# Latent attention in a two-block model: score products split into rounded parts, and a diagonal of inverse sums in the turn of the exponentials

## The chip, the cores and the metric

One core of one Trainium2 chip runs the whole program, from the loads of the weights to the store of the result. The time is device microseconds (us) of one execution. TensorE (PE) multiplies, VectorE (DVE), ScalarE (ACT) and GpSimd (POOL) work elementwise, and SyncE (SP) issues the loads. The engines run side by side, each takes its own instructions in order, and they wait for each other by semaphores. PEld is TensorE's loading of the operand that stays in the array, which can overlap its products.

## The reference, cut to what matters

The model has a first block of two layers and a second, larger one. The change touches one part of each layer of the first block, the latent attention over 512 tokens with 8 heads, and nothing of the second block.

```
q = (rms_norm(c_q, q_norm_g) @ w_uq).reshape(B, S, MLA_HEADS, MLA_NOPE + MLA_ROPE)     # 64 + 32
q_nope, q_rope = q[..., :MLA_NOPE], apply_rope(q[..., MLA_NOPE:], cos, sin)
kv = (rms_norm(c_kv, kv_norm_g) @ w_ukv).reshape(B, S, MLA_HEADS, MLA_NOPE + MLA_V)
k_nope, v = kv[..., :MLA_NOPE], kv[..., MLA_NOPE:]
k_rope = apply_rope(k_r[:, :, None, :], cos, sin)[:, :, 0, :]
s = (einsum('bqhd,bkhd->bhqk', qn, k_nope) + einsum('bqhr,bkr->bhqk', qr, k_rope)) * scale
p = softmax(s, axis=-1)
o = einsum('bhqk,bkhd->bqhd', p, v)
```

All of it is in float32.

## The kernel before, in words

`first_block` runs each layer as stages with a barrier of all engines between them: `project_in`, `dilated_attention`, `mla_attention`, `project_out`. Whatever lengthens a stage's longest engine or chain lengthens the program.

`mla_attention` first makes q and k for all heads: products of halves (`low`, `uq`, `ukv`, in the type float32r, three products each for upper by upper, upper by lower and lower by upper part), a copy of q out of PSUM by ACT (L952), the turn by the rope tables on DVE (`turn`, L992), the inverse norms spread over a tile by a product with the identity (L899), and k times them on DVE (L1020). q and k (`qn`, `kn`, `qr`, `m.kr`) are then plain float32.

The rest of the stage is a loop over 16 units. A unit is a pair of heads (e = 0, 1) and a tile of 128 queries. Per unit:

- `score(u)`, PE: for each head one product over the 64 rows of the nope part (L830) and one over 32 rows of the rope part (L833), 512 keys wide. The two heads lie in different row groups of the array.
- DVE: the maximum (L1024) and the shift (L1025).
- ACT: the exponential with the row sum (L966), twice.
- DVE: the inverse of the sums (L1037) and the exponentials times it (L1039, "evened").
- `flip(u)`, PE: eight transposes of 128x128 (L852).
- ACT: copy of the transposed tiles out of PSUM (L974), twice.
- `mix(u)`, PE: sixteen short products with v (eight calls, L865).

PE's own order in the loop is written out by hand: `score(u + 1)`, `mix(u - 1)`, `flip(u)`. ACT's is the exponentials of u, then the copies of u - 1. DVE has, between the shift and the inverse of each unit, a quarter of a pair's `ada.fold` (class `Modulations`, L528 and L531): a vector times a weight matrix that a later stage needs. Its weights come in eight chunks of 1 MB per layer through a ring of four slots; SP issues the load of chunk n when the chunk that had the slot is folded (L509, L510). The unit with i == 1 also has one multiplication into `m.mix` (L1033), and after units 5, 9 and 13 PE sums the folded pair (`ada.sum`, L541).

Ahead of the loop PE runs score(0), value(0), value(1), score(1), value(2), value(3), where `value` makes v (L840) and ACT copies it out (L957).

Of the kernel before, what the change touches and what calls it, by code (L numbers as in the profile page):

```python
# [16 lines left out]
F32 = mybir.dt.float32  # L17
# [474 lines left out]
class Modulations:  # L492
# [6 lines left out]
    def __init__(self, nc, m, c, sem, layer, part, bank, held=2):  # L499
        self.nc, self.m, self.layer, self.part, self.bank, self.held = nc, m, layer, part, bank, held  # L500
        self.ring = c.enter_context(nc.sbuf_tensor(f"ada{part}_ring", [P, 4, KD, WC], F32))
        self.acc = c.enter_context(nc.sbuf_tensor(f"ada{part}_acc", [P, held, 2, WC], F32))
        self.loaded = [sem(f"ada_loaded{i}") for i in range(4)]
        self.own, self.folded, self.summed = sem("ada_own"), sem("ada_folded"), sem("ada_summed")

    def load(self, sp, chunks=range(ADA_CHUNKS)):
        for n in chunks:
            if n >= 4:
                sp.wait_ge(self.folded, n - 3)  # L509
            sp.dma_start(self.ring[:, n % 4], self.m.ada_w[bass.ds(self.layer, 1), self.part, n].rearrange(  # L510
                "l p k w -> p (l k) w")).then_inc(self.loaded[n % 4], 16)

    def fold(self, dve, pair, ks=range(KD)):
# [10 lines left out]
        for k in ks:  # L524
            for i in range(2):
                acc, w = self.acc[:, pair % self.held, i], self.ring[:, (2 * pair + i) % 4, k]
# [227 lines left out]
def mla_attention(nc, m, layer, gains):  # L754
# [6 lines left out]
    with stage(nc, "mla") as sem, ExitStack() as c:  # L761
# [5 lines left out]
        qn, qr = sb("qn", [P, PAIRS, T]), sb("qr", [P, 2, T])  # L767
# [3 lines left out]
        tmp, inv, spread = sb("tmp", [P, T]), sb("inv", [P, T]), sb("spread", [P, TT, P])  # L771
        rms, q_scale, q_minus = sb("rms", [P, 2, TT]), sb("q_scale", [P, TT]), sb("q_minus", [P, TT])
# [10 lines left out]
        ada = Modulations(nc, m, c, sem, layer, 1, m.ps[:, 7])  # L783
# [12 lines left out]
        with nc.Block(no_gpsimd_drain=True) as block:  # L796
# [14 lines left out]
            def _(pe):  # L811
                def score(u):
                    pair, i, s = u // TT, u % TT, 2 * (u % 2)
                    if u == 0:
                        pe.wait_ge(taken, 3)
                        pe.wait_ge(turned, 2)
                    elif i == 0:
                        pe.wait_ge(taken, 3 + pair)
                    if u == 2 * TT:
                        pe.wait_ge(turned, 3)  # L820
                    if i == 0:
                        pe.wait_ge(keyed, pair + 1)
# [5 lines left out]
                    for e in range(2):  # L828
                        h = halves(e)
                        nc.tensor.matmul(m.ps[:, s + e], qn[h, pair, at], kn[h, pair], start=True, stop=False)  # L830
                    for e in range(2):
                        r = slice(64 * e + 32 * (pair % 2), 64 * e + 32 * (pair % 2) + ROPE)
                        mm = nc.tensor.matmul(m.ps[:, s + e], qr[r, pair // 2, at], m.kr[r], start=False, stop=True)  # L833
# [2092 lines left out]
```

## Time and profile before

| | |
|---|---|
| median of 3 runs | 3000.61 us (2998.66 to 3001.7) |
| the profiled execution's own time | 2992.54 us |
| its span | 2990.7 us |
| share of the span: PE, PEld, DVE, ACT | 88%, 71%, 53%, 32% |
| mean granted TensorE clock | 0.917 of 2.4 GHz |
| latent attention, first work to last, first layer | 422.8 to 537.4 us |
| the same, second layer | about 1007 to 1127 us |

A share is an average over stages with different limits. The two stretches of latent attention together are some 235 us, 8% of the span. A float32 product stands in the trace as two records of PE, a float32r product and a transpose as one each.

### The profile page before, as it was taken

What the parts mean: (1) busy time and instruction counts of PE and PEld (TensorE: products, weight loads), DVE (VectorE), ACT (ScalarE), POOL (GpSimd) and SP (SyncE); (2) the same over time, 40 slices, a digit from 0 to 9 for tenths busy, and PEclk for the clock granted to TensorE, in tenths of its full rate; (3) what the DMA queues carried; (4) which work ended last, traced back from release to release, by engine and by line L of the source; (5) the groups of instructions that cost most, each with busy time, mean ns of one, the idle gap of its engine ahead of it and who ended that gap; (6) DMA issues with size and microseconds to landing.
All of it is one profiled execution on the core that took longest, in us unless ns stands there. A gap on an engine that the chain in (4) does not pass through costs nothing. (4 is left out here: it accounts for less than half of the span.)

```text
span 2990.7 us, 45168 instructions
## 1 busy us (share of the span) xinstructions
PE 2618.2 (88%) x19036; PEld 2109.0 (71%) x19036; DVE 1597.7 (53%) x2352; ACT 945.8 (32%) x1401; POOL 188.5 (6%) x163
## 2 busy tenths in 40 slices
PE   8999899889998998898663989589999892899998
PEld 7888675778886757687562878478878761688877
DVE  3473478835725687444556656644552348455532
ACT  4223135432231353423223333233332321433321
POOL 0000000200000002000001322010001000100001
PEclk9999999989999998899566999799999896899999
DMA  4332231423313214221001000222322120232231
GB/s 129 98 99 78 95 123 64 169 93 99 93 63 116 101 64 176 81 96 62 0 0 56 4 3 4 78 74 95 99 104 107 50 66 0 85 100 98 97 116 48
DMA packets 55958, 237.93 MB, mean 80 GB/s; under 512 B 6545, under 2 KB 7185, under 8 KB 47185
## 3 DMA queue, kind: packets, MB, share of 16 engines
q1 hardware_dynamic: 55760, 235.10, 23.3%
q8 instruction: 149, 2.44, 0.3%
q14 instruction: 49, 0.39, 0.0%
HBM read 230.88 MB, written 4.19 MB: 79 GB/s over the span
## 5 line engine op out<-in xcount | busy, mean ns | idle before, releaser
L341 PE MATMUL banks<-b_h,pin_pair 128*128 128x512 f32 x2304 | 528.3, 390 | 0.0
L341 PEld LDWEIGHTS banks<-b_h,pin_pair 128*128 128x128 f32 x2304 | 431.2, 188 | 88.9
L341 PE MATMUL banks<-ffh,ff_pair 128*128 128x512 f32 x2016 | 457.3, 389 | 0.0
L341 PEld LDWEIGHTS banks<-ffh,ff_pair 128*128 128x128 f32 x2016 | 378.4, 188 | 78.6
L341 PE MATMUL banks<-b_h,pab_pair 128*128 128x512 f32 x792 | 182.4, 393 | 8.0 <-DVE pab_pair L327 8.0
L341 PEld LDWEIGHTS banks<-b_h,pab_pair 128*128 128x128 f32 x792 | 149.9, 190 | 39.4 <-DVE pab_pair L327 8.2
L531 DVE SCALAR_TENSOR_TENSOR ada_acc<-ada_ring,sc,ada_acc 128x256 f32<-128x256 f32 x336 | 158.2, 538 | 0.0
L2558 DVE TENSOR_TENSOR ff<-ff_c,ff 128x512 fp32r<-128x512 f32 x44 | 30.5, 693 | 204.8 <-ACT ff L2546 203.4
L327 DVE TENSOR_TENSOR pin_pair<-pin_raw,pin_pair 128x1024 fp32r<-128x1024 f32 x50 | 61.3, 1226 | 141.4 <-ACT pin_pair L320 141.4
L1134 DVE SCALAR_TENSOR_TENSOR x<-banks,modf,x 128x512 f32<-128x512 f32 x32 | 24.0, 751 | 206.8 <-PE banks L359 206.8
L327 DVE TENSOR_TENSOR pin_pair<-first,pin_pair 128x1024 fp32r<-128x1024 f32 x50 | 61.3, 1226 | 125.2 <-ACT pin_pair L320 125.2
L320 ACT ACTIVATE ff_pair<-ff_raw 128x1024 fp32r<-128x1024 f32 x58 | 61.4, 1059 | 182.4 <-PE banks L341 182.4
L352 PE MATMUL banks<-ff,dn_pair 128*128 128x512 f32 x352 | 87.5, 406 | 13.9 <-ACT dn_pair L320 13.9
L352 PEld LDWEIGHTS banks<-ff,dn_pair 128*128 128x128 f32 x352 | 69.5, 198 | 29.6 <-ACT dn_pair L320 14.7
L320 ACT ACTIVATE dn_pair<-dn_raw 128x2816 fp32r<-128x2816 f32 x16 | 40.9, 2557 | 153.0 <-PE banks L359 142.1
L750 ACT ACTIVATE dil_pt<-banks 128x1024 f32<-128x1024 f32 x32 | 32.8, 1025 | 168.3 <-PE banks L676 168.3
L359 PE MATMUL banks<-ff,dn_pair 128*128 128x512 f32 x352 | 82.4, 389 | 0.0
L356 PE MATMUL banks<-ff,dn_pair 128*128 128x512 f32 x352 | 82.4, 389 | 0.0
L2256 DVE COPY_PREDICATED ru_inv<-rw_levels,banks 128x512 f32<-128x512 uint32 (+1 forms) x80 | 53.7, 676 | 53.2 <-PE banks L2085 52.7
L2686 DVE SCALAR_TENSOR_TENSOR fc_acc<-b_hb,params,fc_acc 128x512 f32<-128x512 f32 x116 | 76.9, 737 | 0.0
L356 PEld LDWEIGHTS banks<-ff,dn_pair 128*128 128x128 f32 x352 | 66.1, 188 | 13.7
L359 PEld LDWEIGHTS banks<-ff,dn_pair 128*128 128x128 f32 x352 | 66.1, 188 | 13.7
(496 smaller groups left out, 4604.2 us busy)
## 6 DMA issues: line engine op xcount, KB each, us to landing
ada_ring<-in_ada_w SPq DMA_DIRECT2D x48, 1024.0 KB, 7.8
ff_raw<-in_ffn_up SPq DMA_DIRECT2D x58, 512.0 KB, 3.7
pin_raw<-in_w_in SPq DMA_DIRECT2D x50, 512.0 KB, 3.6
first<-in_w_in SPq DMA_DIRECT2D x48, 512.0 KB, 3.6
dn_raw<-in_ffn_down SPq DMA_DIRECT2D x16, 1408.0 KB, 6.1
first<-in_ffn_up SPq DMA_DIRECT2D x30, 512.0 KB, 3.7
pab_raw<-in_ab_in SPq DMA_DIRECT2D x23, 512.0 KB, 3.5
out_raw<-in_w_out SPq DMA_DIRECT2D x12, 512.0 KB, 8.9
```

What stands on the lines that cost most here:

```text
L320: nc.scalar.activation(pair[:, t % slots, 0], ring.at(t), ACT.Copy).then_inc(rounded, 1)
L327: nc.vector.tensor_tensor(pair[:, t % slots, 1], ring.at(t), pair[:, t % slots, 0].bitcast(F32), ALU.subtract).then_inc(split, 1)
L341: mm = nc.tensor.matmul(bank, w(a, k), x(b, k), start=k == 0 and i == 0, stop=k == kt - 1 and i == 2)
L352: nc.tensor.matmul(bank, w(0, k), x(0, k), start=k == 0, stop=False)
L356: nc.tensor.matmul(bank, w(0, k), x(1, k), start=False, stop=False)
L359: mm = nc.tensor.matmul(bank, w(1, k), x(0, k), start=False, stop=k == kt - 1)
L531: ins = nc.vector.scalar_tensor_tensor(acc, w, self.m.sc[:, k:k + 1], acc, ALU.mult, ALU.add)
L750: nc.scalar.activation(pt[:, s:s + 2], m.ps[:, s:s + 2], ACT.Exp, scale=scale)\
L1134: ins = nc.vector.scalar_tensor_tensor(m.x[:, j], m.ps[:, j % 4], gate[:, j:j + 1], m.x[:, j], ALU.mult, ALU.add)
L2256: nc.vector.copy_predicated(inv[:, i % 2, f:2, e], over(m.levels[:, d, l, f:2]), m.ps[:, 4 + e, 2 * f * P:].rearrange("p (k t n) -> p k t ...
L2558: chain.step(nc.vector.tensor_tensor(ff[:, 1, j], cv[:, j % 2], ff[:, 0, j].bitcast(F32), ALU.subtract))
L2686: nc.vector.scalar_tensor_tensor(acc[:, k], hb[:, k, bass.ds(tap, T)], w[:, bass.ds(4 * tap + k, 1)], acc[:, k], ALU.mult, ALU.add).then_i ...
```

## The change

The scores: q and k are each split into an upper part (ACT copies the number into float32r, which rounds it) and a lower one (DVE subtracts the upper from the whole). Each float32 product becomes three float32r products, (upper, upper), (upper, lower), (lower, upper). The parts of k lie over `uq`, the parts of the rope pieces over `low`, both of which are no longer needed then.

The turn: DVE no longer multiplies the 128x512 exponentials by the inverse sums. It multiplies the 128x128 identity by them, and the eight transposes become eight float32 products of the exponentials with that diagonal.

The ring of the weight chunks in this stage has three slots in place of four.

```
-    def __init__(self, nc, m, c, sem, layer, part, bank, held=2):
+    def __init__(self, nc, m, c, sem, layer, part, bank, held=2, slots=4):
...
-            if n >= 4:
-                sp.wait_ge(self.folded, n - 3)
+            if n >= self.slots:
+                sp.wait_ge(self.folded, n - self.slots + 1)
...
-        qn, qr = sb("qn", [P, PAIRS, T]), sb("qr", [P, 2, T])
+        qn, qr = sb("qn", [P, 2, PAIRS, T], F32R), sb("qr", [P, 2, T])
+        kn_half = uq[:].rearrange("p a k n -> p (a k n)")[:, 0:2 * PAIRS * T].rearrange(
+            "p (a j n) -> p a j n", a=2, j=PAIRS)
+        kr_half, qr_half = low[:, :, 0], low[:, :, 1:3]
+        diag = spread[:].rearrange("p (u e) n -> p u e n", u=2)
-        ada = Modulations(nc, m, c, sem, layer, 1, m.ps[:, 7])
+        ada = Modulations(nc, m, c, sem, layer, 1, m.ps[:, 7], slots=3)
 # PE, score(u)
                     if u == 0:
-                        pe.wait_ge(taken, 3)
-                        pe.wait_ge(turned, 2)
+                        pe.wait_ge(rope_lower, 2)
+                    if u <= 1:
+                        pe.wait_ge(q_lower, PAIRS if u else 2)
                     if i == 0:
-                        pe.wait_ge(keyed, pair + 1)
+                        pe.wait_ge(k_lower, pair + 1)
-                    for e in range(2):
-                        h = halves(e)
-                        nc.tensor.matmul(m.ps[:, s + e], qn[h, pair, at], kn[h, pair], start=True, stop=False)
-                    for e in range(2):
-                        r = slice(64 * e + 32 * (pair % 2), 64 * e + 32 * (pair % 2) + ROPE)
-                        mm = nc.tensor.matmul(m.ps[:, s + e], qr[r, pair // 2, at], m.kr[r], start=False, stop=True)
+                    passes = ((0, 0), (0, 1), (1, 0))
+                    for a, b in passes:
+                        for e in range(2):
+                            h = halves(e)
+                            nc.tensor.matmul(m.ps[:, s + e], qn[h, a, pair, at], kn_half[h, b, pair],
+                                             start=(a, b) == passes[0], stop=False)
+                    for a, b in passes:
+                        for e in range(2):
+                            r = slice(64 * e + 32 * (pair % 2), 64 * e + 32 * (pair % 2) + ROPE)
+                            mm = nc.tensor.matmul(m.ps[:, s + e], qr_half[r, a, pair // 2, at], kr_half[r, b],
+                                                  start=False, stop=(a, b) == passes[2])
 # PE, flip(u)
-                            mm = nc.tensor.transpose(m.ps[:, 4 + e, j * P:j * P + P],
-                                                     ex[:, 2 * (u % 2) + e, j * P:j * P + P], m.ident[:])
+                            mm = nc.tensor.matmul(m.ps[:, 4 + e, j * P:j * P + P],
+                                                  ex[:, 2 * (u % 2) + e, j * P:j * P + P], diag[:, u % 2, e],
+                                                  start=j == 0, stop=j == TT - 1, skip_group_check=True)
 # PE, the products that make k
                     if j >= 2:
-                        pe.wait_ge(taken, j + 1)
+                        pe.wait_ge(q_lower, j - 1)
 # ACT, after the copy of the spread norms
+                act.wait_ge(turned, 1)
+                nc.scalar.activation(kr_half[:, 0], m.kr[:], ACT.Copy).then_inc(rope_upper, 1)
+                act.wait_ge(turned, 2)
+                nc.scalar.activation(qr_half[:, 0, 0], qr[:, 0], ACT.Copy).then_inc(rope_upper, 1)
+                for j in range(PAIRS):
+                    act.wait_ge(keyed, j + 1)
+                    nc.scalar.activation(kn_half[:, 0, j], kn[:, j], ACT.Copy).then_inc(k_upper, 1)
...
+                    if u == 2:
+                        act.wait_ge(turned, 3)
+                        nc.scalar.activation(qr_half[:, 0, 1], qr[:, 1], ACT.Copy).then_inc(rope_upper, 1)
 # DVE
+                def lower_rope(n, half, whole):
+                    dve.wait_ge(rope_upper, n + 1)
+                    nc.vector.tensor_tensor(half[:, 1], whole, half[:, 0].bitcast(F32), ALU.subtract)\
+                        .then_inc(rope_lower, 1)
...
                 turn(qr[:, 0])
+                lower_rope(0, kr_half, m.kr[:])
+                for t in range(PAIRS):
+                    dve.wait_ge(taken, 3 + t)
+                    nc.vector.tensor_tensor(qn[:, 1, t], m.ps[:, 2 + t], qn[:, 0, t].bitcast(F32), ALU.subtract)\
+                        .then_inc(q_lower, 1)
+                lower_rope(1, qr_half[:, :, 0], qr[:, 0])
...
                     nc.vector.tensor_tensor(kn[:, j], m.ps[:, k_bank(j)], inv[:], ALU.mult).then_inc(keyed, 1)
+                for j in range(PAIRS):
+                    dve.wait_ge(k_upper, j + 1)
+                    nc.vector.tensor_tensor(kn_half[:, 1, j], kn[:, j], kn_half[:, 0, j].bitcast(F32), ALU.subtract)\
+                        .then_inc(k_lower, 1)
...
+                    if u == 2:
+                        lower_rope(2, qr_half[:, :, 1], qr[:, 1])
...
                     for e in range(2):
-                        nc.vector.tensor_scalar(ex[:, s + e], ex[:, s + e], total[:, u % 2, e:e + 1], None, ALU.mult)\
-                            .then_inc(evened, 1)
+                        if u >= 2:
+                            dve.wait_ge(flipped, 2 * u + e - 3)
+                        nc.vector.tensor_scalar(diag[:, u % 2, e], m.ident[:], total[:, u % 2, e:e + 1], None,
+                                                ALU.mult).then_inc(evened, 1)
```

How the instructions stand, on the two engines that the loop waits for. First PE from score(1) into the loop, before: L830 and L833 are the scores, L840 makes v, L852 is the turn, L865 the products with v. The last number of a row is the count of calls.

```order
L830 MATMUL banks<-mla_raw,mla_qn 128x512 x2
L833 MATMUL banks<-b_kr,mla_qr 128x512 x2
L840 MATMUL banks<-mla_ukv,mla_low 128x512 x12
L852 MATMUL banks<-ident,mla_work 128x128 x8
L830 MATMUL banks<-mla_raw,mla_qn 128x512 x2
L833 MATMUL banks<-b_kr,mla_qr 128x512 x2
L865 MATMUL banks<-mla_work,mla_raw 64x128 x8
```

The same place after, where L839 and L844 are the scores (the upper and lower parts lie in `mla_uq` and `mla_low`), L852 makes v, L864 is the turn with the diagonal (in `mla_spread`) and L878 the products with v.

```order
L839 MATMUL banks<-mla_uq,mla_qn 128x512 x6
L844 MATMUL banks<-mla_low 128x512 x6
L852 MATMUL banks<-mla_ukv,mla_low 128x512 x12
L864 MATMUL banks<-mla_spread,mla_work 128x128 x8
L839 MATMUL banks<-mla_uq,mla_qn 128x512 x6
L844 MATMUL banks<-mla_low 128x512 x6
L878 MATMUL banks<-mla_work,mla_raw 64x128 x8
```

The order of the groups is the same; a score has twelve calls where it had four, and the turn keeps eight calls of another kind.

Now DVE from the end of the rope turn of the first q tile to the first maximum, before. L303 is the last step of a turn, L1020 is k times the norms, L1024 the maximum, L1025 the shift.

```order
L302 TENSOR_TENSOR mla_qr<-mla_qr,mla_cos 128x512
L303 TENSOR_TENSOR mla_qr<-mla_qr,mla_tmp 128x512
L1020 TENSOR_TENSOR mla_raw<-banks,mla_inv 128x512 x4
L1024 TENSOR_REDUCE mla_top<-banks 128x2
L1025 TENSOR_SCALAR mla_shift<-mla_top,mla_q_minus 128x2
```

And after: L1018 makes a lower rope part, L1049 the lower parts of q, L1055 is k times the norms, L1058 makes the lower parts of k, L1063 is the maximum.

```order
L303 TENSOR_TENSOR mla_qr<-mla_qr,mla_tmp 128x512
L1018 TENSOR_TENSOR mla_low<-b_kr,mla_low 128x512
L1049 TENSOR_TENSOR mla_qn<-banks,mla_qn 128x512 x4
L1018 TENSOR_TENSOR mla_low<-mla_qr,mla_low 128x512
L1055 TENSOR_TENSOR mla_raw<-banks,mla_inv 128x512 x4
L1058 TENSOR_TENSOR mla_uq<-mla_raw,mla_uq 128x512 x4
L1063 TENSOR_REDUCE mla_top<-banks 128x2
```

Ten subtractions have come in ahead of the first maximum; score(0) on PE waits for the first seven of them and for all four multiplications of k.

## Rows read from the trace of the kernel before

**Rows 1.** The page: busy time, share and instructions of each engine.
```profile
PE 2618.2 (88%) x19036; PEld 2109.0 (71%) x19036; DVE 1597.7 (53%) x2352; ACT 945.8 (32%) x1401; POOL 188.5 (6%) x163
```
**Rows 2.** The windows view, loops of both layers; PEclk is the granted clock.
```profile
core 0: us, PE busy (x) PEld busy (x) DVE busy (x) ACT busy (x) POOL busy (x), PEclk, DMA share, GB/s
469.10:530.00 60.90, 59.99 (x468) 34.69 (x467) 56.26 (x127) 35.45 (x83) 0.00 (x0) 1.00 0.21 79
1059.60:1120.00 60.40, 57.85 (x451) 33.51 (x451) 54.50 (x124) 35.25 (x82) 0.00 (x0) 1.00 0.21 79
```
**Rows 3.** The timeline, PE, one unit: start, duration, engine, line, xrecords.
```profile
476.35 1.13 PE L830 MATMUL banks<-mla_raw,mla_qn 64*128 64x512 f32 x4
477.41 1.13 PE L833 MATMUL banks<-b_kr,mla_qr 32*128 32x512 f32 x4
478.48 1.09 PE L865 MATMUL banks<-mla_work,mla_raw 128*64 128x128 f32 x16
479.51 1.09 PE L852 MATMUL banks<-ident,mla_work 128*128 128x128 f32 x8
480.53 1.13 PE L830 MATMUL banks<-mla_raw,mla_qn 64*128 64x512 f32 x4
```
**Rows 4.** The timeline, DVE and ACT, the same unit; idle time in brackets.
```profile
478.59 1.23 DVE L1024 TENSOR_REDUCE mla_top<-banks 128x2 f32<-128x1024 f32 x1
479.98 0.61 DVE L528 TENSOR_SCALAR ada_acc<-ada_ring,sc 128x256 f32<-128x256 f32 x2
480.11 0.78 ACT L966 ACTIVATE mla_work<-banks,mla_shift,mla_q_scale 128x512 f32<-128x512 f32 x1 [1.68 <-DVE mla_shift L1025]
481.64 1.08 ACT L974 ACTIVATE mla_work<-banks 128x512 f32<-128x512 f32 x2
481.77 0.17 DVE L1037 RECIPROCAL mla_total<-mla_total 128x2 f32<-128x2 f32 x1 [0.39 <-ACT mla_work L966]
481.97 0.88 DVE L1039 TENSOR_SCALAR mla_work<-mla_work,mla_total 128x512 f32<-128x512 f32 x2
```
**Rows 5.** The timeline, PE weight loads: score(3) and the last score, first layer.
```profile
472.05 0.30 PEld L830 LDWEIGHTS banks<-mla_raw,mla_qn 64*128 64x128 f32 x4 [0.17 <-issue]
525.21 0.30 PEld L830 LDWEIGHTS banks<-mla_raw,mla_qn 64*128 64x128 f32 x4
```
**Rows 6.** The timeline ahead of the loop: float32r and float32 products, a small scaling.
```profile
436.92 0.86 DVE L1007 TENSOR_SCALAR mla_spread<-ones,mla_rms 128x128 f32<-128x128 f32 x4
435.90 8.47 PE L892 MATMUL banks<-mla_low,mla_uq 128*128 128x512 f32 x36
443.99 1.08 PEld L899 LDWEIGHTS banks<-ident,mla_spread 128*128 128x128 f32 x8
444.99 5.30 PEld L911 LDWEIGHTS banks<-mla_low,mla_ukv 128*128 128x128 f32 x24
```
**Rows 7.** The timeline, the start of the first layer's loop.
```profile
446.80 0.68 DVE L1020 TENSOR_TENSOR mla_raw<-banks,mla_inv 128x512 f32<-128x512 f32 x1
450.64 0.30 PEld L830 LDWEIGHTS banks<-mla_raw,mla_qn 64*128 64x128 f32 x4 [0.35 <-issue]
460.87 0.69 ACT L957 ACTIVATE mla_raw<-banks,mla_rms 128x512 f32<-128x512 f32 x1 [0.67 <-PE banks L840]
462.88 0.78 ACT L966 ACTIVATE mla_work<-banks,mla_shift,mla_q_scale 128x512 f32<-128x512 f32 x1
465.28 1.61 PE L852 MATMUL banks<-ident,mla_work 128*128 128x128 f32 x8 [4.44 <-DVE mla_work L1039]
```
**Rows 8.** The timeline, the last turn of the first layer.
```profile
532.65 1.09 PE L852 MATMUL banks<-ident,mla_work 128*128 128x128 f32 x8
```
**Rows 9.** The tile view of the ring, 476.9 to 477.4 us: one load.
```profile
L510 SPq DMA_DIRECT2D ada_ring<-in_ada_w x1: 333/333/333, 477.1 to 477.1; - x1
DMA to landing us min/median/max: 4.8/4.8/4.8
```
**Rows 10.** The windows view, stretches at the lower clock in and behind both loops.
```profile
465.70:469.10 3.40, 3.40 (x13) 1.57 (x12) 3.21 (x8) 2.05 (x6) 0.00 (x0) 0.50 0.02 5
1049.40:1059.60 10.20, 8.78 (x37) 5.11 (x38) 7.75 (x18) 4.48 (x11) 0.00 (x0) 0.50 0.01 2
537.40:544.20 6.80, 4.70 (x10) 2.88 (x11) 5.42 (x8) 6.17 (x10) 0.00 (x0) 0.50 0.77 277
1121.10:1134.70 13.60, 9.98 (x41) 7.36 (x40) 6.51 (x11) 7.36 (x12) 0.00 (x0) 0.50 0.40 149
```

More of the change, by code:

```diff
@@ L497 @@
     PAIRS = ADA_CHUNKS // 2
-    def __init__(self, nc, m, c, sem, layer, part, bank, held=2):
+    def __init__(self, nc, m, c, sem, layer, part, bank, held=2, slots=4):
         self.nc, self.m, self.layer, self.part, self.bank, self.held = nc, m, layer, part, bank, held
-        self.ring = c.enter_context(nc.sbuf_tensor(f"ada{part}_ring", [P, 4, KD, WC], F32))
+        self.slots = slots
+        self.ring = c.enter_context(nc.sbuf_tensor(f"ada{part}_ring", [P, slots, KD, WC], F32))
         self.acc = c.enter_context(nc.sbuf_tensor(f"ada{part}_acc", [P, held, 2, WC], F32))
-        self.loaded = [sem(f"ada_loaded{i}") for i in range(4)]
+        self.loaded = [sem(f"ada_loaded{i}") for i in range(slots)]
         self.own, self.folded, self.summed = sem("ada_own"), sem("ada_folded"), sem("ada_summed")
@@ L507, in load @@
         for n in chunks:
-            if n >= 4:
-                sp.wait_ge(self.folded, n - 3)
-            sp.dma_start(self.ring[:, n % 4], self.m.ada_w[bass.ds(self.layer, 1), self.part, n].rearrange(
-                "l p k w -> p (l k) w")).then_inc(self.loaded[n % 4], 16)
+            if n >= self.slots:
+                sp.wait_ge(self.folded, n - self.slots + 1)
+            sp.dma_start(self.ring[:, n % self.slots], self.m.ada_w[bass.ds(self.layer, 1), self.part, n].rearrange(
+                "l p k w -> p (l k) w")).then_inc(self.loaded[n % self.slots], 16)
     def fold(self, dve, pair, ks=range(KD)):
@@ L525, in fold @@
             for i in range(2):
-                acc, w = self.acc[:, pair % self.held, i], self.ring[:, (2 * pair + i) % 4, k]
+                acc, w = self.acc[:, pair % self.held, i], self.ring[:, (2 * pair + i) % self.slots, k]
                 if k == 0:
@@ L766, in mla_attention @@
         low = sb("low", [P, 2, nq + nkv, T], F32R)
-        qn, qr = sb("qn", [P, PAIRS, T]), sb("qr", [P, 2, T])
+        qn, qr = sb("qn", [P, 2, PAIRS, T], F32R), sb("qr", [P, 2, T])
+        kn_half = uq[:].rearrange("p a k n -> p (a k n)")[:, 0:2 * PAIRS * T].rearrange(
+            "p (a j n) -> p a j n", a=2, j=PAIRS)
+        kr_half, qr_half = low[:, :, 0], low[:, :, 1:3]
+        q_lower, rope_upper, rope_lower, k_upper = (
+            sem(x) for x in ("q_lower", "rope_upper", "rope_lower", "k_upper"))
+        k_lower = sem("k_lower")
         v, kn = (raw[:, n * TT * T:(n + 1) * TT * T].rearrange("p (j n) -> p j n", j=TT) for n in range(2))
@@ L814, in score @@
                     if u == 0:
-                        pe.wait_ge(taken, 3)
-                        pe.wait_ge(turned, 2)
-                    elif i == 0:
-                        pe.wait_ge(taken, 3 + pair)
+                        pe.wait_ge(rope_lower, 2)
+                    if u <= 1:
+                        pe.wait_ge(q_lower, PAIRS if u else 2)
                     if u == 2 * TT:
-                        pe.wait_ge(turned, 3)
+                        pe.wait_ge(rope_lower, 3)
                     if i == 0:
-                        pe.wait_ge(keyed, pair + 1)
+                        pe.wait_ge(k_lower, pair + 1)
                     if u == 1:
@@ L951, in _ @@
                     act.wait_ge(made, t + 1)
-                    nc.scalar.activation(qr[:, t] if t < 2 else qn[:, t - 2], m.ps[:, t], ACT.Copy).then_inc(taken, 1)
+                    nc.scalar.activation(qr[:, t] if t < 2 else qn[:, 0, t - 2], m.ps[:, t], ACT.Copy)\
+                        .then_inc(taken, 1)
                 act.wait_ge(stretched, 1)
                 nc.scalar.activation(inv[:], m.ps[:, 7], ACT.Copy).then_inc(spread_in, 1)
+                act.wait_ge(turned, 1)
[5 more added lines that the diff above has]
+                    nc.scalar.activation(kn_half[:, 0, j], kn[:, j], ACT.Copy).then_inc(k_upper, 1)
                 for i in range(TT):
```

## The prediction

> **What bounds the kernel now.** I read the page's busy shares first, then the windows of the two loops, then the timeline of one unit engine by engine, and last the starts and ends of the stage. TensorE is busy 88% of the span [rows 1], which says little of this stage; the windows do: in both loops of the latent attention PE is busy 96 to 98% at the full clock, DVE over 90%, ACT under 60% [rows 2]. The timeline of a unit shows PE without a hole: the nope scores start at 476.35, the rope scores 1.06 us later, the products with v 1.07 after that, the turn 1.03 later, the next score 1.02 later; 4.18 us in all [rows 3]. The reader is to see the second thing, too: DVE and ACT run almost as long a cycle. Counted from the end of the score (478.48), the maximum starts at +0.11, the fold at +1.50, the exponentials at +1.63, the copies run from +3.16 to +4.24, the inverse stands at +3.29, and the two multiplications of the exponentials end at +4.37 [rows 4]. So the loop has two nearly equal bounds, and the change lengthens one and shortens the other. From score(3) to the last score there are twelve intervals in 53.16 us [rows 5], 4.43 each, since three of them hold an `ada.sum` of PE's. The rest of the program isn't touched.
>
> **The scores.** A float32 product is two records, and the two heads' products lie in different row groups: four records of 512 columns take 1.06 us [rows 3]. Two heads side by side would need 2 x 2 x 512 columns at 2.4 GHz, 0.85 us, so 0.21 us are left for the first weight load and the change of tile shape. The float32r products of the q projection take one record each, and 36 of them go from 435.90 to 443.99, 0.225 us each [rows 6]. They use all 128 rows; no row shows float32r products of 64 or 32 rows. I take the value by which they pair up as the float32 ones do, since the calls alternate e = 0 and e = 1 and lie in different banks: three rounds of 0.225 plus 0.21 make 0.885 us in place of 1.06. Both kinds of score together: 1.77 in place of 2.13, a saving of 0.36 us. The lower bound is rounds of 0.213, a saving of 0.43; the upper is that the heads go one after the other, twelve times 0.225 plus 0.42, 3.12 us, 0.99 us more than before.
>
> A rule speaks against my value. The hidden loads show in the rows: 36 full-height products with 36 loads pass at 0.225 us each, with one load of 128 columns behind every one of them [rows 6]. The Trainium skill, page "TensorE: Matmul & The Clock Gate", Part 3, says that a weight load overlaps a running product only when its row group differs. By that rule the second and third round of each score show their loads and the saving is gone; by the row it stands. The trace contradicts the rule for full height, and shows nothing for half height in float32r. I keep it as rival A.
>
> **The turn.** Eight transposes, one record each, take 1.02 us [rows 3]. The product that spreads the norms has the form of the new turn (float32, 128x128 against a 128x128 moving tile): eight records for four products, 1.00 us from its first load to the next product's [rows 6], of which about 0.11 is the change, so 0.111 a record. Eight products are sixteen records, eight more than now: +0.89, with the slightly longer records of this form +0.91 us. The unit on PE becomes 4.18 - 0.36 + 0.91 = 4.73 us.
>
> **DVE and ACT in the loop.** Scaling four 128x128 tiles took 0.86 us [rows 6], so a diagonal costs 0.22 and the two 0.43 in place of 0.88. They end at +3.92 in place of +4.37, and the next score ends at +4.73: DVE gets 0.8 us of slack. The copies end at +4.24 and the products with v may start at +4.73: 0.49 us of slack. The saving on DVE is therefore worth nothing; its cover is PE's longer unit. The new wait of DVE on `flipped` is for the turn two units back, long done. The single subtraction and copy of the third rope piece at u = 2 (0.69 and 0.6 us) fit into the slack but for 0.1 or 0.2 us.
>
> **The ring of three.** Chunk 3 can be asked for only when chunk 0 is folded, near the end of unit 3, where it was there from the start; the same for chunks 5 and 7 at units 7 and 11. The next fold waits for it, and behind that wait on DVE stand the inverse, the diagonal and the next maximum. A load issued in this place landed 4.8 us later [rows 9]. The chunk is free about 1.3 us into the fold, so it is there 1.3 + 0.2 + 4.8 = 6.3 us after that fold began, and the next fold comes 4.73 after it: DVE stands for 1.6 us. The fold then ends at 1.50 + 1.6 + 1.5 = +4.6, the diagonals at +5.25. The turn wants them at 4.73 + 1.03 = +5.76: in time. The next maximum is 0.4 us late, the copies have 0.49: also in time. Price 0, with nothing left; each us by which a chunk comes later costs a us at six places.
>
> **The start of the loop.** Score(0) waits for seven new subtractions and four multiplications on DVE. From 446.80, eleven operations of 0.68 plus 0.03 between them [rows 7] end at 454.8 by steps of 0.72; before, score(0) started at 450.64 [rows 7], since the multiplications were waiting for PE anyway. That is +4.2. PE gets back 2 x 0.36 on scores 0 and 1: the last v copy (460.87) and the first exponential (462.88) [rows 7] come 3.5 later. The first turn (465.28) waits for half a multiplication before and a diagonal now, 0.26 less: +3.2. The other three subtractions of k and ACT's six copies lie beside score(0) and the products for v.
>
> **The sum, per layer.** Start +3.2. First turn +1.2 (0.91, but part of it at the lower clock, which began at 465.70 and 1049.40 [rows 10]). Interval from score(2) to score(3), at the lower clock in part, +0.7. Twelve intervals of +0.55, less some 0.3 us that PE waits now: +6.3. End: last score -0.36, last turn (532.65 [rows 8]) +0.91, both on the path: +0.5. Together 11.9, and 23.8 for two layers. Against the profiled execution: 2992.5 + 23.8 = 3016.3. The median of the runs shown lies 8.1 above that execution, and I forecast medians: 3000.6 + 23.8 = 3024.
>
> **The rivals.**
> A, the loads show. Four rounds a unit pay half of the 0.21, about 0.11, and are 0.213 long otherwise: +0.36 a unit, sixteen units, two layers, +11.5: 3036. For it: nothing in float32r at half height is in the trace. Against: the full-height row.
> B, the heads go one after the other in float32r: 1.35 a unit more than forecast, +43: 3067. Against: the float32 products of the same shape do pair up.
> C, the chunks come later than 4.8 us after the issue: 2 us more at six places, +12: 3036. The slack is used up by my own sum, which speaks for it; that two loads issued 0.5 us apart share the same engines is in the 4.8 already.
> D, the clock gives it back, which would end without a loss. The place is the start and end of both loops: 3.4, 10.2, 6.8 and 13.6 us stand at half clock [rows 10], 34 us, of which all with PE work would be worth half, 17 us: 3007; with rounds of 0.213 in all units 2.3 less, 3005, within the measurement. It decides from about 18 us given back. For it: the turns become true products, and the first half-clock stretch begins in a turn. Against: both loops ran at the full clock for 60 us with transposes in them [rows 2], and the idle time ahead of the first turn stays. The Trainium skill, same page, Part 4, says that transposes don't count as work for the clock as products do. By that rule the new turns would help to hold the clock; the trace shows no lower clock in a running loop that they could lift.
> E, the clock takes more. PE has nothing to do between the end of k's products, about 451.1, and 454.8. The idle 4.4 us ahead of the first turn [rows 7] was followed by a lower clock [rows 10]; if this new hole is too, 3.4 us at half clock cost 1.7 a layer and 10.2 cost 5: 3028 to 3034.
>
> **How the numbers follow.** Forecast 0.57 (its own range 3016 to 3033), E 0.15, A 0.09, B 0.08, C 0.05, D 0.06. The range of 3012 to 3042 takes in the forecast, E, A and C, alone and A with E; B and D stay out. What a measurement of this kernel can tell from no change is about 0.2%, 6 us. Half of D and a little luck in the forecast's low end make 0.04 for the same, 0.03 for faster; all else is slower, 0.93.
>
> **What would show it.** In the profile after: the nope and rope scores start 0.88 us apart, not 1.06 (A), not 1.5 (B). The turns show sixteen records and 1.93 us. Starts of scores in the loop are 4.73 us apart, PE over 97% busy there. The first turn comes 3.2 us later in its stage. DVE stands 1.6 us ahead of the fold at units 4, 8 and 12 and PE doesn't. Granted clock in both loops 1.00. The forecast is wrong if the time is under 3012, if PE waits in the loop, or if the scores are longer than 1.77 us.

## The result, and the profile after

The changed kernel takes 3023.91 us (median of 4, 3020.27 to 3026.57), the kernel before on the same chip 2999.64 (median of 4, 2997.69 to 3001.7). The ratio is 1.008, with an interval of 1.0063 to 1.0097: slower by 24.3 us, where 24 was forecast. The profiled execution has a span of 3024.8 us.

The page, busy time by engine, answers to [rows 1]: PE has 22 us more, DVE 1 and ACT 8.

```profile
PE 2640.0 (87%) x19382; PEld 2160.4 (71%) x19420; DVE 1598.8 (53%) x2374; ACT 954.3 (32%) x1415; POOL 188.3 (6%) x163
```

The windows of both loops answer to [rows 2], with the same columns: PE 97% busy, DVE down from 92% to 71% in the first layer, the granted clock 1.00 in both. The 3% are two waits behind the last score (540.45); up to there PE doesn't stand.

```profile
477.50:551.00 73.50, 71.59 (x674) 56.68 (x674) 52.45 (x130) 37.67 (x86) 0.00 (x0) 1.00 0.21 80
1078.30:1151.80 73.50, 71.59 (x674) 56.66 (x674) 52.46 (x130) 37.67 (x86) 0.00 (x0) 1.00 0.22 80
```

The timeline of PE, one unit, answers to [rows 3]. L839 and L844 are the nope and rope scores, L878 the products with v, L864 the turn.

```profile
485.32 0.97 PE L839 MATMUL banks<-mla_uq,mla_qn 64*128 64x512 f32 x6
486.22 0.96 PE L844 MATMUL banks<-mla_low 32*128 32x512 f32 x6
487.11 1.09 PE L878 MATMUL banks<-mla_work,mla_raw 128*64 128x128 f32 x16
488.13 2.05 PE L864 MATMUL banks<-mla_spread,mla_work 128*128 128x128 f32 x16
490.12 0.96 PE L839 MATMUL banks<-mla_uq,mla_qn 64*128 64x512 f32 x6
```

From start to start that is 0.90, 0.89, 1.02 and 1.99 us, a unit of 4.80 where it was 4.18. There is no idle time in brackets: PE has no hole. The six records of a score stand for three rounds of two heads, the sixteen of the turn for eight float32 products.

DVE and ACT around the same unit, at the fold whose chunk comes late (they answer to [rows 4]):

```profile
490.31 0.62 DVE L529 TENSOR_SCALAR ada_acc<-ada_ring,sc 128x256 f32<-128x256 f32 x2 [1.60 <-DMA ada_ring<-in_ada_w]
490.27 1.08 ACT L998 ACTIVATE mla_work<-banks 128x512 f32<-128x512 f32 x2
491.83 0.48 DVE L1082 TENSOR_SCALAR mla_spread<-ident,mla_total 128x128 f32<-128x128 f32 x2
491.90 1.09 PE L878 MATMUL banks<-mla_work,mla_raw 128*64 128x128 f32 x16
492.92 2.05 PE L864 MATMUL banks<-mla_spread,mla_work 128*128 128x128 f32 x16
```

DVE stood for 1.60 us, yet the diagonals (491.83, 0.48 long) are done 0.6 us before the turn starts. The first layer's waits of DVE on the ring, from the view of waits (us in total, times, longest):

```profile
DVE ada_acc L529 <- DMA ada_ring<-in_ada_w: 4.7, 3, 1.6
```

The timeline of the start of the loop answers to [rows 7]:

```profile
448.49 0.68 DVE L1018 TENSOR_TENSOR mla_low<-b_kr,mla_low 128x512 fp32r<-128x512 f32 x1
449.09 2.48 DVE L1049 TENSOR_TENSOR mla_qn<-banks,mla_qn 128x512 fp32r<-128x512 f32 x4
451.48 0.68 DVE L1018 TENSOR_TENSOR mla_low<-mla_qr,mla_low 128x512 fp32r<-128x512 f32 x1
452.08 2.48 DVE L1055 TENSOR_TENSOR mla_raw<-banks,mla_inv 128x512 f32<-128x512 f32 x4
454.48 2.49 DVE L1058 TENSOR_TENSOR mla_uq<-mla_raw,mla_uq 128x512 fp32r<-128x512 f32 x4
455.27 0.90 PEld L839 LDWEIGHTS banks<-mla_uq,mla_qn 64*128 64x128 f32 x6 [2.86 <-issue]
```

The first lower part of k (454.48) is the last of the eleven DVE operations, counted from 448.49, that score(0) needs; score(0) starts 0.79 us behind its start. The eleven step by 0.60 us. The windows of the two stretches at the lower clock in this layer, same columns as above (they answer to [rows 10]):

```profile
455.40:462.20 6.80, 6.80 (x21) 4.60 (x22) 5.14 (x10) 0.69 (x1) 0.00 (x0) 0.50 0.00 0
472.50:475.90 3.40, 3.40 (x18) 3.17 (x18) 3.21 (x9) 2.17 (x6) 0.00 (x0) 0.50 0.02 5
```

The first begins with score(0), behind a hole on PE: for 2.86 us it loaded no weights, for 2.46 it ran no product. Before, there was no such stretch at this place. The second begins in the first turn, as before.

From the barrier ahead of the latent attention to the one behind it, the two layers took 114.9 and 121.0 us before, and 130.6 and 130.5 after: +15.6 and +9.5, 25.1 together. By the prediction's terms, in us:

| term | forecast, a layer | layer 1 | layer 2 |
|---|---|---|---|
| up to the first copy of q (unchanged code) | 0 | +1.5 | 0.0 |
| from there to score(0) | +4.2 | +3.0 | +3.0 |
| score(0) to the first turn | -1.0 | +2.2 | +2.2 |
| first turn to score(2) | +1.2 | +1.9 | +1.7 |
| score(2) to score(3) | +0.7 | -0.4 | -2.6 |
| twelve intervals | +6.3 | +6.8 | +6.8 |
| last score to the end | +0.5 | +0.6 | -1.6 |
| sum | 11.9 | 15.6 | 9.5 |

The +1.5 is not the change's. In the 26 layers of all the profiles of this document, the way from the start of the stage to the first copy of q takes 18.2 to 18.3 us where the clock is at half for 10.2 us around the stage's start, and 19.5 to 19.7 where it is so for 13.7. The kernel before had 10.2 in its first layer and 13.7 in its second, the changed kernel 13.7 in both.

The profiled spans differ by 34.1 us, the medians by 24.3. Of the 34.1, 9.0 lie outside the two stages, in code that is the same; single executions scatter by that much (the kernel before alone ran in 2976.8 to 2998.3 us on one chip). So below, stages and units are read from profiles, and medians only beside the runs of the kernel before on the same chip.

### The profile page after: what moved, and what is told of

The parts are those of the page before. It is cut to its first block and busy times, and to the rows that moved or that the text cites. A ratio compares the mean times of both kernels' runs of the same rounds, so it can differ in the third digit from the quotient of the medians.

```text
span 3024.8 us, 45962 instructions
## 1 busy us (share of the span) xinstructions
PE 2640.0 (87%) x19382; PEld 2160.4 (71%) x19420; DVE 1598.8 (53%) x2374; ACT 954.3 (32%) x1415; POOL 188.3 (6%) x163
## 3 DMA queue, kind: packets, MB, share of 16 engines
HBM read 230.88 MB, written 4.19 MB: 78 GB/s over the span
## 5 line engine op out<-in xcount | busy, mean ns | idle before, releaser
L352 PEld LDWEIGHTS banks<-ff,dn_pair 128*128 128x128 f32 x352 | 69.5, 198 | 29.7 <-ACT dn_pair L320 14.7
L864 PE MATMUL banks<-mla_spread,mla_work 128*128 128x128 f32 x512 | 68.7, 290 | 8.5 <-DVE mla_spread L1082 8.5
L359 PEld LDWEIGHTS banks<-ff,dn_pair 128*128 128x128 f32 x352 | 66.1, 188 | 13.7
```

Of the source, the lines that this page charges most:

```text
L352: nc.tensor.matmul(bank, w(0, k), x(0, k), start=k == 0, stop=False)
L359: mm = nc.tensor.matmul(bank, w(1, k), x(0, k), start=False, stop=k == kt - 1)
L864: mm = nc.tensor.matmul(m.ps[:, 4 + e, j * P:j * P + P], ex[:, 2 * (u % 2) + e, j * P:j * P + P], diag[:, u % 2, e], start=j == 0, stop=j ...
```

## The experiments

Two edits come back below: the old turn (the exponentials scaled by DVE, then transposed) and a ring of four.

**The scores alone.** The changed kernel with the old turn, the ring still three chunks long.

```diff
-                            mm = nc.tensor.matmul(m.ps[:, 4 + e, j * P:j * P + P],
-                                                  ex[:, 2 * (u % 2) + e, j * P:j * P + P], diag[:, u % 2, e],
-                                                  start=j == 0, stop=j == TT - 1, skip_group_check=True)
+                            mm = nc.tensor.transpose(m.ps[:, 4 + e, j * P:j * P + P],
+                                                     ex[:, 2 * (u % 2) + e, j * P:j * P + P], m.ident[:])
...
-                        nc.vector.tensor_scalar(diag[:, u % 2, e], m.ident[:], total[:, u % 2, e:e + 1], None,
-                                                ALU.mult).then_inc(evened, 1)
+                        nc.vector.tensor_scalar(ex[:, s + e], ex[:, s + e], total[:, u % 2, e:e + 1], None, ALU.mult)\
+                            .then_inc(evened, 1)
```

> The changed kernel with the old turn: DVE multiplies the exponentials, PE transposes; scores in three rounds and ring of three stay. Theory (the new turn is PE's cost, the split scores save a third of a us a unit there): PE's share of a unit falls from 4.79 to 3.84 us, so PE no longer bounds; DVE with ACT does, at 4.28 us a unit, and now the late chunks show, 6.3 - 4.28 = 2.0 us at six places. Start of the loop +3 a layer. Together about +8 a layer, 3014 to 3019 us where before is 3000, turns of eight records in 1.02 us. Rival (the turn is free, since DVE wins what PE loses, and start and splitting cost the 24 us): as slow as the changed kernel or slower, 3024 or more. Second rival (the turn is all of it): no slower than before, 3000 or less.

Measured: 3016.63 against 2990.91 us, ratio 1.0096 [1.0075, 1.0117]; stages of 128.0 and 129.2 us. From one maximum on DVE to the next, a unit takes 4.18 us where the chunk is there, but 5.8 to 5.9 where it is late and the clock stays. The timeline of PE at such a place, and the windows ahead of it and behind it:

```profile
490.01 1.48 PE L876 MATMUL banks<-mla_work,mla_raw 128*64 128x128 f32 x16 [1.55 <-ACT mla_work L996]
```
```profile
472.00:483.50 11.50, 10.54 (x98) 7.18 (x93) 9.11 (x21) 7.26 (x18) 0.00 (x0) 1.00 0.33 123
485.50:490.00 4.50, 2.88 (x20) 1.82 (x20) 4.43 (x11) 2.60 (x6) 0.00 (x0) 1.00 0.02 5
490.60:500.80 10.20, 10.20 (x59) 8.03 (x56) 6.55 (x15) 3.80 (x9) 0.00 (x0) 0.50 0.00 0
```

With the shorter unit of PE the late chunk reaches PE: 1.55 us of idle time here. Behind it, in the middle of the loop, stands a stretch at half the clock (0.50 for 10.2 us), in which one interval took 7.7 us. The two layers have six waits of 1.54 or 1.55 us in this place: behind this one the clock is at half for 10.2 us, at four others for 3.4, and at one, ahead of 512.93, not at all. That made this kernel slower than I expected; the scores' own saving can't be read from it.

**The turn alone.** The kernel before with the new turn; scores in float32, ring of four.

> The kernel before with the new turn alone: diagonal on DVE, eight float32 products on PE; float32 scores, ring of four. Theory: PE's unit is 4.18 + 0.95 = 5.13 us; twelve intervals of +0.95, first and last turn and the slow-clock unit +3: +14 a layer, about 3028 us, more than the whole change costs. Rival (turn free): within 6 us of before. Second rival (turn is all of the 24 us, scores nothing): 3024.

Measured: 3015.21 against 2990.91 us, ratio 1.0084 [1.0066, 1.0102]. The timeline of PE:

```profile
484.29 1.09 PE L867 MATMUL banks<-mla_work,mla_raw 128*64 128x128 f32 x16
485.31 2.05 PE L853 MATMUL banks<-mla_spread,mla_work 128*128 128x128 f32 x16
487.29 1.13 PE L831 MATMUL banks<-mla_raw,mla_qn 64*128 64x512 f32 x4
489.41 1.09 PE L867 MATMUL banks<-mla_work,mla_raw 128*64 128x128 f32 x16
```

A unit is 5.12 us, 0.94 more than before, all of it in the turn (485.31 to 487.29 is 1.98 us). The stages take 130.8 and 130.7 us, those of the changed kernel 130.6 and 130.5: the turn alone costs as much as the whole change.

**The ring alone.** The kernel before with three chunks.

```diff
-        ada = Modulations(nc, m, c, sem, layer, 1, m.ps[:, 7])
+        ada = Modulations(nc, m, c, sem, layer, 1, m.ps[:, 7], slots=3)
```

> The kernel before with three slots in place of four in this stage's ring, nothing else. Theory: the load of chunks 3, 5 and 7 lands about 6.3 us after the fold that frees the slot began, the next fold comes 4.2 us after it: DVE stands 2.1 us, and here neither DVE nor PE has slack for it, so 1.5 to 2 us each pass on, six places, +9 to +12 us. In the changed kernel the same wait (1.6 us) is covered by PE's longer unit. Rival (the ring is hidden here too): within 3 us of before, PE's units unchanged at 4.18 to 4.30.

Measured: 2998.41 against 2990.91 us, ratio 1.003 [1.0016, 1.0043], 7.5 us where 9 to 12 were expected. In layer 1 the view of waits has DVE on the ring for 6.4 us, at most 2.2 at a time, and three intervals of the loop are 5.75 to 6.02 us where they were 4.19 to 4.28. PE at the first of them:

```profile
488.64 1.09 PE L866 MATMUL banks<-mla_work,mla_raw 128*64 128x128 f32 x16 [1.22 <-ACT mla_work L975]
```

DVE is late with its scalings, so ACT is late with its copies, and PE stands. The cover that the prediction named was therefore needed: without PE's longer unit the ring costs some 8 us (the twelve intervals are 4.9 and 4.8 us longer in the two layers).

**The change again, on the same chip as the three that follow.** No edit.

> The changed kernel once more, on the chip of the next three, so that they can be compared with it. All theories: 0.8% over before, 24 us, units of 4.79 us.

Measured: 3017.62 against 2987.54 us, ratio 1.0103 [1.0079, 1.0128]; stages of 127.7 and 130.5 us. The timeline, score(0), and the windows of the lower clock in layer 1:

```profile
451.09 0.56 PEld L839 LDWEIGHTS banks<-mla_uq,mla_qn 64*128 64x128 f32 x6 [2.85 <-issue]
```
```profile
453.00:456.40 3.40, 3.40 (x8) 2.65 (x9) 3.30 (x6) 0.60 (x1) 0.00 (x0) 0.51 0.00 0
466.70:470.10 3.40, 3.40 (x16) 3.17 (x16) 3.21 (x8) 2.01 (x5) 0.00 (x0) 0.50 0.02 5
```

The two layers of one execution differ in how long the lower clock lasts behind score(0): 3.4 us here, 6.8 in its second layer. The stages differ by 2.8 us: 1.3 up to the first copy of q and 1.5 from score(0) to the first turn.

Here the change costs 30.1 us, at the first measurement it cost 24.3.

**The change with a ring of four.** The fourth chunk lies in the half of `raw` that k leaves, and k in `pt`.

```diff
-        ada = Modulations(nc, m, c, sem, layer, 1, m.ps[:, 7], slots=3)
+        ada = Modulations(nc, m, c, sem, layer, 1, m.ps[:, 7],
+                          spare=(raw[:, TT * T:2 * TT * T].rearrange("p (k w) -> p k w", k=KD), (fine, nq + nkv)))
```

> The changed kernel with four slots again; the fourth lies over the raw weights, whose halves are made by then, and k before its split lies where the turned exponentials go later. Theory (in the changed kernel the late chunks are covered by PE's longer unit): DVE's three waits of 1.6 us a layer go and nothing else moves, 0 to -1 us against the changed kernel. Rival (they cost there what they cost in the kernel before with a ring of three): 8 to 10 us less.

Measured: 3018.69 against 2987.54 us (the change 3017.62), ratio 1.0103 [1.0079, 1.0128]; stages of 130.6 and 130.5 us. DVE no longer waits for the ring, and PE's unit is the same 4.79 us:

```profile
488.61 0.96 PE L847 MATMUL banks<-mla_uq,mla_qn 64*128 64x512 f32 x6
493.40 0.96 PE L847 MATMUL banks<-mla_uq,mla_qn 64*128 64x512 f32 x6
```

The twelve intervals take 59.9 us with either ring. So in the changed kernel the ring of three costs nothing that can be measured.

**The scores alone, with a ring of four.** Both edits together.

> The split scores alone, with the old turn and four slots: the change without its new turn and without its ring. Theory: PE needs 3.84 us a unit, DVE with ACT 4.28, so a group of four units takes 17.6 to 17.8 us as in the kernel before, and PE's saving is worth nothing; no waits for chunks; the start costs 3 us a layer, the last score gives 0.35 back: +5 us over before, 1.002. If the lower clock returns in the loop although DVE has no late chunks, PE's idle time of 0.4 us a unit alone is enough for it; then +10. Rival (split scores pay): 0.3 us a unit off, -5 or less. Rival (splitting itself is dear): +15 or more.

Measured: 2995.07 against 2987.54 us, ratio 1.003 [1.0016, 1.0044]; stages of 119.0 and 118.9 us. Four units take 17.26 us, before 17.72, and the window of the loop shows who bounds now: DVE is busy 95% and PE 93%.

```profile
472.00:530.00 58.00, 54.19 (x505) 38.51 (x500) 54.88 (x126) 34.78 (x81) 0.00 (x0) 1.00 0.22 83
```
```profile
488.26 1.09 PE L884 MATMUL banks<-mla_work,mla_raw 128*64 128x128 f32 x16 [0.27 <-ACT mla_work L1004]
```

PE's work in a unit is 0.34 us shorter, but in three of four units 0.26 to 0.38 us come back as a wait for ACT's copies; these stand behind exponentials that waited for DVE. What is left, some 0.1 us a unit, doesn't pay for the start of the loop.

**The start of the loop.** The changed kernel, with DVE working on what score(0) needs first: half of the lower parts of q, then one tile of k with its lower part.

```diff
+                lower_q(0)
+                lower_q(1)
+                dve.wait_ge(spread_in, 1)
+                whole_k(0)
+                lower_rope(1, qr_half[:, :, 0], qr[:, 0])
+                lower_k(0)
+                lower_q(2)
+                lower_q(3)
+                for j in range(1, PAIRS):
+                    whole_k(j)
+                for j in range(1, PAIRS):
+                    lower_k(j)
```

> The changed kernel with another order on DVE ahead of the loop: only the subtractions that score(0) needs come first (two parts of q, the first multiplication of k, the second rope part, the first lower part of k), the other seven operations behind them; the products for v wait for the parts of q that lie in their banks. Theory (the start costs 4 us because score(0) stands behind eleven operations): score(0) comes 2.5 to 2.9 us earlier in its stage and the loop with it, 5 to 6 us less than the changed kernel. Rival (the start is bound by the copies of v or the first exponential, whatever score(0) does): the first turn stays where it is, 0. Rival (what the start loses is the clock): the slow stretch behind score(0) goes and 3 us more come back in each layer.

Measured: 3004.89 against 2987.54 us, ratio 1.0064 [1.0039, 1.0089], 12.7 us less than the change on this chip; stages of 123.5 and 126.0 us, 4.2 and 4.5 less. The timeline and windows:

```profile
448.09 0.53 PEld L839 LDWEIGHTS banks<-mla_uq,mla_qn 64*128 64x128 f32 x6 [0.35 <-issue]
```
```profile
448.10:462.70 14.60, 10.36 (x55) 7.02 (x55) 10.93 (x23) 7.50 (x12) 0.00 (x0) 1.00 0.00 0
462.80:466.20 3.40, 3.40 (x17) 2.84 (x16) 2.88 (x9) 2.67 (x7) 0.00 (x0) 0.52 0.02 5
```

Score(0) starts 3.0 us earlier, 2.6 counted from the stage's start, and with the hole ahead of it (0.35 for 2.85 us) the lower clock behind it is gone: 1.00 up to the first turn, in which the stretch of 3.4 us stands as ever. The last score moves by 4.2 us: 2.6 from the order, the rest from the clock. The loop's unit stays at 4.80. The two stages give 8.7 of the 12.7 us; the rest lies where the code is the same.

**The two heads one after the other.** The loop over heads goes outside the loop over products.

```diff
-                    for a, b in passes:
-                        for e in range(2):
+                    for e in range(2):
+                        for a, b in passes:
```

> The changed kernel with the two loops of a score exchanged: first the three rounds of head 0, then those of head 1, so that neighbours mostly share a row group. Theory (float32r products pair up because neighbours lie in different row groups, and products start in order): only the last of head 0 and the first of head 1 run side by side, five rounds of 0.225 us in place of three, +0.45 a score kind, +0.9 a unit, +29 us over the changed kernel. Rival (all six in a row once the order is lost): +1.35 a unit, +43. Rival (the order is of no account): 0.

Measured: 3012.44 against 2990.01 us, ratio 1.008 [1.0057, 1.0102]; a unit is 4.81 us where it was 4.79. My theory had 0.9 us more a unit, and fell. The timeline of PE in a stretch of 0.13 us, 484.95 to 485.08:

```profile
484.96 0.50 PE L839 MATMUL banks<-mla_uq,mla_qn 64*128 64x512 f32 x2
```

Two products start there 10 ns apart, and the next two 0.33 us later. The records don't name the head. I take the second for head 1's, though two more products of head 0 stand between them in the program, since the six products take as long as with alternating calls. So the heads' products seem to run side by side whatever the order of the calls; what is measured is that the order costs nothing.

**Two products for three.** The product of q's lower with k's upper part is left out, which prices one round.

```diff
-                    passes = ((0, 0), (0, 1), (1, 0))
+                    passes = ((0, 0), (0, 1))
```

> The changed kernel without the products of q's lower part with k's upper part, two rounds a score kind in place of three. Theory: PE bounds the loop, a round costs 0.225 us, so 0.45 a unit less, -14 us against the changed kernel; units of 4.34 us. The DVE waits for chunks grow to 2.0 us and begin to pass through in part, +2. Rival (another engine bounds the unit): less than 5 us off. Rival (rounds show their weight loads): 0.33 a round, -21.

Measured: 3008.63 against 2990.01 us, ratio 1.006 [1.0037, 1.0084]. A unit is 4.33 us, so a round is 0.23. The saving in time was expected at 14 us; against the run above, whose unit is 4.81, it is 3.8. The twelve intervals take 57.2 and 57.6 us, 2.8 and 2.5 less than there, where twelve shorter units alone would save 5.8: the late chunks pass through at this length.

```profile
487.81 0.73 PE L839 MATMUL banks<-mla_uq,mla_qn 64*128 64x512 f32 x4
492.24 0.73 PE L839 MATMUL banks<-mla_uq,mla_qn 64*128 64x512 f32 x4
494.48 1.09 PE L878 MATMUL banks<-mla_work,mla_raw 128*64 128x128 f32 x16 [0.85 <-ACT mla_work L998]
```

With 4.33 us PE waits 0.85 at such a unit, with 4.79 not at all: the cover ends between the two.

**Split scores, the old turn, ring of four, short start.** What the runs so far recommend.

> Split scores with the old turn, a ring of four and the shorter start: what the runs so far show as the cheapest parts together, with both multiplications on DVE. Theory: groups of four units at 17.25 us as with the split scores and the ring of four (17.72 in the kernel before), three of them 1.4 us off a layer; the first maximum in the loop 0.5 us earlier than before; the last score 0.35: 2 us a layer, 4 in all, 0.9985; no lower clock behind score(0). Rival (the clock decides: each layer's start runs 3.4 or 10.2 us at half clock by chance, worth up to 5 us): no difference that can be told, 0.9985 to 1.0015 with stages between 113 and 119 us. Rival (the two effects don't add, since the earlier start only moves the wait to the copies of v): as with the split scores and a ring of four, 1.003.

Measured: 2990.85 against 2992.67 us, ratio 0.9997 [0.998, 1.0014]; stages of 114.4 and 118.2 us. No difference from the kernel before can be told.

**The same with one scaling on ACT.** ACT scales head 1's exponentials, so that DVE's cycle is shorter.

```diff
+                        nc.scalar.activation(ex[:, s + 1], ex[:, s + 1], ACT.Copy, scale=total[:, u % 2, 1:2])\
+                            .then_inc(evened_b, 1)
```

> A version meant to beat both: split scores, old turn by transposes, ring of four, the shorter start, and of the two multiplications of the exponentials one on DVE and one on ACT behind its copies. Theory: PE needs 3.84 us a unit, DVE 3.84, and the copies end 4.24 us after the score, which makes units of 4.04; a group of four units with its sum 17.0 us in place of 17.7; start +0.6, end -0.35: 2 us a layer less than before, -4 us, 0.9985. If PE's idle time in the loop brings the lower clock back, +3 to +6 instead. Rival (ACT becomes the bound with 3.5 us busy and its waits): units of 4.9, +20.

Measured: 2989.16 against 2990.01 us, ratio 1.000 [0.9985, 1.0015]. Four units take 17.05 us, 0.2 less than with both on DVE, which is too little to show in the time. In half of the units PE still waits for ACT's copies; here they stand behind exponentials that waited 1.06 us for DVE:

```profile
488.04 1.09 PE L884 MATMUL banks<-mla_work,mla_raw 128*64 128x128 f32 x16 [0.36 <-ACT mla_work L1004]
```

None of these versions beats the kernel before by what can be measured.

## Why the prediction was right

**What bounds the loop** was right and decides the sign. PE had no hole in the loop before; its unit grew from 4.18 to 4.79 us (forecast 4.73), and DVE's shorter work bought nothing.

**The scores** were forecast at 1.77 us for both kinds and took 1.79: rounds of 0.23 and two starts. By the letter of the prediction's own signs ("longer than 1.77 us") that is a miss, of 0.02. Rival A, that the loads of the second and third round show, is out: a score would be 1.07 us long, and it is 0.90; the price of one round, taken by leaving one out, is 0.23. By the rule of the Trainium skill that the prediction weighed ("TensorE: Matmul & The Clock Gate", Part 3) these loads, in the same row group as the product before them, should not have overlapped; the trace disagrees for half height, too, with rounds 0.23 us apart. The same part of the Trainium skill makes an exception for a load into a background weight buffer; no record here says which buffer a load goes to. Rival B is out by the same row; and with heads called one after the other it didn't come either.

**The turn** was forecast at 1.93 and took 1.98: 16 records of 0.111 and the change of shape. Put in alone, it cost 0.94 us a unit against the forecast's 0.91. That and the scores, 0.05 and 0.02 us over the forecast, make the twelve intervals +6.8 us for +6.3.

**The ring** was forecast to make DVE stand 1.6 us and to cost nothing: the longest stand is 1.6, PE has none, and a fourth chunk changes nothing. Rival C did not come. That the price was nothing only because of PE's longer unit is shown from both sides: the ring of three in the kernel before cost 1.6 to 1.7 us at each place, and with units of 4.33 PE waited again.

**The start** was mis-sized twice, in opposite directions. The step "eleven operations by steps of 0.72" was wrong (its own 0.68 and 0.03 make 0.71): operations of DVE that don't depend on each other step by 0.60, so score(0) came 3.0 us later instead of 4.2. And rival E, with a chance of 0.15, came true: the hole ahead of score(0) was followed by 6.8 us at half the clock, and the stretch from score(0) to the first turn grew by 2.2 us instead of shrinking by 1.0. With the short start and no lower clock it is 13.9 us, 0.8 less than before; with 3.4 us at half clock it is 15.4, with 6.8 it is 16.9. The sign "the first turn comes 3.2 us later in its stage" failed with it: it came 6.7 and 5.3 later. All seven profiles with the hole show such a stretch in both layers, 3.4 or 6.8 us long; the three with the short start show none in any of their six layers, nor do the three without split scores. So the hole is shown to be the cause. Its length went with that of the stretch at the lower clock at the very start of the stage: 3.4 where that one was 10.2 us, 6.8 where it was 13.7, in all fourteen layers. What ties the two together, and what sets the first, stays open.

**The rest of the stage** lent luck. In the kernel before, its second layer had 10.2 us at half the clock around the first turns and 13.6 behind the loop [rows 10]; after, there are 3.4 in the first turn and none before the closing barrier. So score(2) to score(3) and the end came out 3.3 and 2.1 us under the forecast there, and took back what E and the 1.5 us of unchanged code ahead of the loop in layer 1 had cost. The stage sums to 25.1 for a forecast of 23.8. The mechanism and the terms of the loop hold; the match within a microsecond is partly chance, and the repeat of the change, 30.1 us above the kernel before, shows how much: inside the forecast's range, but 6 us off its number. Rival D named a place, too, the start and the end of the loops, and some of it came in layer 2; but the repeat has 3.4 us behind score(0) and 3.4 in the first turn again, and the whole stayed far from its 3005. The Trainium skill (same page, Part 4) says that transposes don't count as work for the clock; where PE waited for 0.7 us at most (split scores, ring of four), the loop with transposes held 1.00 for 58 us, as the one with products does, so no run here shows an effect of it.

The sum of the parts also explains why the whole is no dearer than the turn. Split scores save PE 0.33 us of the turn's 0.94 in a unit, since with the turn in place PE is the bound and every bit saved counts; what they save in sixteen units, 5.3 us a layer, they pay at the start of the loop (3.0 us up to score(0), and the lower clock behind it).

## What to carry to other kernels

Before moving work from one engine to another, compare the lengths of their cycles in one unit: here DVE gave up 0.40 us that were covered and PE, without a hole, took 0.94 that weren't. The price of a split product is its rounds, counted by records and row groups, and the work that makes the parts ahead of the loop, where it also opens a hole for the clock. A shorter ring of buffers costs nothing while the late chunk's lateness is under the slack of the engine behind it, so it is to be priced anew after every change of the bound.

## What the runs showed of the hardware that I had not expected

- With the heads' products called one head after the other, records still start in pairs 10 ns apart and the unit stays at 4.81 us. So products of different row groups seem not to start in the order of the program; which head a record belongs to is inferred.
- Independent operations of DVE on 128x512 elements last 0.68 us each in the records but step by 0.60; one that needs the result of the one before (the last of a rope turn) starts 0.72 after it.
- A wait of PE in the middle of a busy loop (1.55 us, in a stretch of 4.5 us in which PE was busy for 2.9) was followed by 10.2 us at half the clock; of five more of this length in the same kernel, four went with 3.4 us at half the clock and one with none. A late buffer can thus cost several times its own lateness. In the kernel with the ring alone, none of the waits of 1.22 us in the loop was followed by one.
- How long the clock stays low at the start of the stage, 10.2 or 13.7 us, differs between layers of one execution and costs 1.3 us up to the first copy of q; behind a hole it goes with 1.5 us more.
